# RG-LRU gates: square roots by GpSimd's power, block by block, instead of one ScalarE pass for each scan

## What is computed

```
r, i  = sigmoid(gates of xr)                       # per direction
log_a = -RG_C * r * softplus(-rg_lambda)
a     = exp(log_a)
b     = sqrt(-expm1(2 * log_a)) * (i * xr)
h[t]  = a[t] * h[t-1] + b[t]                       # forwards and backwards
```

## Time and profile before

| | before |
|---|---|
| median of 3 runs | 2858.34 us (2851.83 to 2863.38) |
| the profiled execution | 2857.44 us, span 2855.7 us |
| TensorE busy | 2570.2 us, 90% of the span |
| VectorE busy | 1701.7 us, 60% |
| ScalarE busy | 1007.8 us, 35% |
| GpSimd busy | 445.5 us, 16% |
| mean granted TensorE clock | 0.951 of full speed |

### The profile page before, as it was taken

One profiled execution on the slowest core, in us unless ns is written; L12 is line 12 of the kernel. 1 busy time (PEld: TensorE's weight loads), 2 busy tenths in 40 slices (PEclk: granted clock), 3 DMA queues, 4 the chain that ended last, 5 costly groups with the idle time before them and its releaser, 6 DMA issues.

```text
span 2855.7 us, 37592 instructions
## 1 busy us (share of the span) xinstructions
PE 2570.2 (90%) x14948; PEld 1407.6 (49%) x14948; DVE 1701.7 (60%) x2866; ACT 1007.8 (35%) x1951; POOL 445.5 (16%) x342
## 2 busy tenths in 40 slices
PE   7789999675679898997799799999999999999998
PEld 2344655232376776866445344444444444444443
DVE  5752543767756566745555787787876544444445
ACT  2744443555132232323355533333332222221122
POOL 0400000000653617102233211011110000000000
PEclk8999999887789899998899899999999999999999
DMA  7311111000021222001503434434436412222212
GB/s 209 100 41 41 41 48 27 1 15 22 28 72 46 75 24 69 10 9 60 126 1 126 141 132 140 136 116 140 132 109 239 132 50 81 81 82 81 78 47 72
DMA packets 121625, 227.02 MB, mean 79 GB/s; under 512 B 14281, under 2 KB 59849, under 8 KB 116969
## 3 DMA queue, kind: packets, MB, share of 16 engines
q1 hardware_dynamic: 121448, 224.60, 24.7%
HBM read 162.55 MB, written 61.87 MB: 79 GB/s over the span
## 4 chain that ended last, share of the span: by engine, by line
PE 69%; issue 10%; DVE 8%; POOL 6%; ACT 4%; DMA 1%; SPq 0%; DVEq 0%; POOLq 0%; ACTq 0%
PE pb L2175 23%; PE pb L2117 20%; PE pb L286 8%; PE pb L2097 5%; PE pb L295 2%; POOL arena L1183 2%; POOL arena L1186 1%; DVE arena L1341 1%; POOL arena L1189 1%; PE pb L1776 1%; PE pb L2006 1%; PE pb L525 1%; POOL arena L1207 1%; DVE arena L1443 1%; POOL MS L1200 1%
## 5 line engine op out<-in xcount | busy, mean ns | idle before, releaser
L2175 PE MATMUL pb<-arena 128*128 128x512 f16 x3072 | 667.9, 379 | 0.0
L2117 PE MATMUL pb<-arena 128*128 128x512 f16 (+2 forms) x2736 | 590.6, 378 | 15.2 <-DVE arena L1650 6.6
L2175 PEld LDWEIGHTS pb<-arena 128*128 128x128 f16 x3072 | 300.6, 98 | 362.4
L1740 DVE SCALAR_TENSOR_TENSOR arena<-pb,arena 128x512 f32<-128x512 f32 x512 | 352.2, 690 | 184.6 <-PE pb L2175 183.2
L286 PE MATMUL pb<-arena 128*128 128x512 f16 (+1 forms) x1992 | 423.7, 374 | 21.2 <-ACT arena L970 9.6
L2117 PEld LDWEIGHTS pb<-arena 128*128 128x128 f16 x2736 | 267.9, 99 | 332.9 <-DVE arena L1650 7.1
L286 PEld LDWEIGHTS pb<-arena 128*128 128x128 f16 x1992 | 195.1, 99 | 247.2 <-issue 18.4
L1715 DVE TENSOR_TENSOR arena<-arena,pb 128x512 f32<-128x512 f32 x224 | 149.2, 683 | 251.1 <-PE pb L2117 251.1
L1116 ACT ACTIVATE arena<-arena 128x512 f32<-128x512 f32 x256 | 160.3, 626 | 172.0 <-DVE arena L1715 168.0
L295 PE MATMUL pb<-arena 128*128 128x128 f16 x3264 | 199.7, 222 | 17.3 <-ACT arena L980 11.1
L295 PEld LDWEIGHTS pb<-arena 128*128 128x128 f16 x3264 | 191.9, 99 | 22.4 <-ACT arena L980 11.0
(11 more groups left out here) (292 smaller groups left out, 3192.4 us busy)
## 6 DMA issues: line engine op xcount, KB each, us to landing
arena<-in_mlp_w SPq DMA_DIRECT2D x31, 1024.0 KB, 6.3
w1x<-arena SPq DMA_DIRECT2D x16, 1792.0 KB, 10.6
arena<-w1x SPq DMA_DIRECT2D x16, 1792.0 KB, 9.2
arena<-in_x SPq DMA_DIRECT2D x128, 128.0 KB, 3.8
arena<-in_ada_rest SPq DMA_DIRECT2D x32, 512.0 KB, 3.6
w2x<-arena SPq DMA_DIRECT2D x16, 1024.0 KB, 8.4
arena<-w2x SPq DMA_DIRECT2D x16, 1024.0 KB, 4.9
arena<-in_w_in SPq DMA_DIRECT2D x26, 512.0 KB, 3.9
```

What stands on the lines that cost most here:

```text
L1740: dve.scalar_tensor_tensor(xs, pb[:, 4 + n % 4, :], 1.0 / (WS * AS), xs, ALU.mult, ALU.add).then_inc(S("acc"), 1)
L2117: mm = pe.matmul(pb[:, (7 * g + j) % 4, c], W1P[g % 2][WDEST[a]][0][:, ws, P * k:P * k + P], token_op(b, L // 2, c)[:, k, hs, :], start=(k ...
L2175: mm = pe.matmul(pb[:, 4 + n % 4, :], ACTP[sl][:, 2 * f + th, hs, P * tt:P * tt + P], W2P[sl][:, f, ws, BLK * dh:BLK * dh + BLK], start=(f ...
```

## The change

OM's square root is no longer taken by ScalarE in one pass. GpSimd raises each block of OM to the power 0.5 in place as soon as `rg_om` says that the block is there, and signals `rg_sq` per block (20 times in place of 4). The exponent is a new column `phalf` of 0.5, spread over the block's columns. VectorE multiplies OM by 0.5 * TI block by block too, one block behind: the product of block x - 1 stands behind TI of block x, and the last block's product ahead of the scans. ScalarE's wait for the fifth `rg_om` and its square root are gone.

```diff
@@ kernel scope
+        phalf = sb("phalf", [P, 1])
@@ ScalarE, end of each scan's blocks
-                    act.wait_ge(S("rg_om"), 10 * j + 5 * d + 5)
-                    act.activation(OM, OM, ACT.Sqrt).then_inc(S("rg_sq"), 1)
@@ GpSimd
-            pool.wait_ge(S("pool_init"), 3)
+            pool.memset(phalf[:], 0.5).then_inc(S("pool_init"), 1)
+            pool.wait_ge(S("pool_init"), 4)
...
             pool.memset(view(115, [4 * KB]), 0.0).then_inc(S("rgw_clear"), 1)
+            for v in range(20):
+                b = RORD[v // 5 % 2][v % 5]
+                n, c = (BLK if b < NB else TC), rcols(b)
+                pool.wait_ge(S("rg_om"), v + 1)
+                pool.tensor_tensor(OM[:, c], OM[:, c], phalf[:].broadcast_to([P, n]), ALU.pow).then_inc(S("rg_sq"), 1)
             pool.wait_ge(S("r_rows"), 1)
@@ VectorE
+            def times_root(v, d, x):
+                c = rcols(RORD[d][x])
+                dve.wait_ge(S("rg_sq"), v + 1)
+                ch(dve.scalar_tensor_tensor(OM[:, c], OM[:, c], 0.5, TI[:, c], ALU.mult, ALU.mult))
...
                         ch(dve.scalar_tensor_tensor(TI[:, c], TI[:, c], 1.0, XR[:, c], ALU.add, ALU.mult))
-                    dve.wait_ge(S("rg_sq"), 2 * j + d + 1)
-                    ch(dve.scalar_tensor_tensor(OM, OM, 0.5, TI, ALU.mult, ALU.mult))
+                        if x:
+                            times_root(v - 1, d, x - 1)
+                    times_root(10 * j + 5 * d + 4, d, 4)
```

## The result

The changed kernel takes 4269.8 us (median of 4 runs, 4268.84 to 4273.15) against 2857.7 us before: ratio 1.4952, 95% interval 1.4929 to 1.4975. The direction was as forecast, and its order of size, but the time lies 20 us above the range (3850 to 4250) and 130 us above the forecast of 4140.

What follows compares the result with a forecast made beforehand. The RG-LRU's chain from first OM to scan was taken as the bound, with GpSimd's powers filling it: 2857.4 us plus 1236 for the powers and 46 for VectorE's blocking gave 4139, taken as 4140; range 3850 to 4250 us.

Steps and rivals of the forecast that it cites:

- What bounds the kernel: RG-LRU, last gate block to scan: anything added there moves the kernel's end; 16.4 us from first OM to scan.
- The pace of the power: GpSimd's powers: straight line through one and two columns, 140 ns a column, 72.1 us for 512; 0.80 with or without blocking.
- the 1298 us of the forecast: GpSimd's powers in four scans: 4 x 72.1 + 36.3 = 324.6 us per scan.
- a pace above 150 ns: GpSimd's powers: each column costs over 150 ns; chance 0.04.
- without the blocking: Rival 4: VectorE works freely beside GpSimd's powers, 4093 us; shares the 0.80 of the line with or without blocking.
- Blocking for the whole power: VectorE's two-SBUF-operand operations between powers wait for a whole GpSimd power: 11.7 us a scan, 46 us in all.
- Rival 1: GpSimd's five powers per scan run at a sum's pace, 1.6 us for 512 columns; 2848 us; chance 0.03.
- Rival 2 and 3: GpSimd's powers: several columns together, 35 ns a column, 3174 us, chance 0.13; or 360 ns a column, 6.1 ms.
- The signs that I set: GpSimd trace: 512-column powers about 72 us, wrong under 58 or over 77; GpSimd on chain; about six table loads fewer.

Runs made afterwards that it cites:

- the price list: The kernel before, with useless powers of 1 to 512 columns and varied data, exponents and partitions put into GpSimd's idle time; 2859.9 us.
- the run at a sum's pace: The changed kernel with GpSimd multiplying each block by 0.5 instead of raising it to the power 0.5; 2857.4 us, ratio 0.9995 to before.

## Why the prediction was wrong

- **What bounds the kernel: right.** The stretch from the first OM to the scan is on the chain; the 1412 us all lie there.
- **The pace of the power: the term that was mis-sized.** I took the step from one column to two, 140 ns, for the slope of a straight line through 512. The line holds, and its fixed part of 0.41 us too, but from one column to 512 the price list gives (81.92 - 0.55) / 511 = 159.2 ns a column. That makes 4 x 2304 x 0.0192 = 177 us more than the 1298 us of the forecast: 1475, and GpSimd's busy time shows 1476. The step was the difference of two rows from different lines of the kernel (690 and 550 ns), carried over a factor of 511; the error of 19 ns in it, an eighth, is worth 177 us. Measured side by side, one column and two differ by 154 ns. I noted that part of the 140 ns might not be the loop's and widened the range downwards for that; the other sign had a chance of 0.04 (a pace above 150 ns) and little room: without the blocking the range's upper end of 4250 is 157 ns a column.
- **Blocking for the whole power: wrong here.** It had 46 us in the sum and costs none. The rows that it came from show a product of 1024 columns and a sum of 512; even there VectorE was let go 0.2 us ahead of GpSimd's end (held for 1.52 us of 1.72). A power of 512 columns takes 82 us and lets VectorE go after 0.8. Without the blocking the forecast had been 4093, further off; the two errors had opposite signs, so that 4140 is as near as it is by luck. 4093 + 177 = 4270, and 4269.8 is measured. The page SBUF — State Buffer of the Trainium skill, section "Who interferes with whom", has the shared ports locked for the whole instruction. These runs nearly agree for multiplications (in the run at a sum's pace the product is let go at 527.89, and GpSimd's step ends at 528.03), but not for powers of up to 512 columns nor for two-operand operations beside one of 1024, and the measurement decides.
- **Rival 1, the power at a sum's pace:** the run with multiplications shows it 9 us too cheap, 2857.4 in place of 2848. I had left out that a product beside GpSimd takes 0.72 us more, four times a scan.
- **Rival 2 and 3:** no sign of several columns together up to 2304, nor of 360 ns.
- **The signs that I set:** a power of 512 columns over 77 us was to show the prediction wrong, and it takes 81.9. The sixteen and four powers, the chain on GpSimd, the powers that touch (the sign of no blocking) and six table loads fewer (13 in place of 19) came as written.

## What to carry to other kernels

Before an operation goes to GpSimd, get its price by the column from two lengths that are far apart and near the length wanted; a slope from one column and two, read off different lines, was 12% off, which is nothing at two columns and 177 us here. Where the range hangs on one slope it should leave room on both sides. A cheap-looking function on a few columns (0.55 us for one) says nothing on a tile: 512 columns of power cost 82 us where ScalarE's root took 2.1 us for 2304. Work on GpSimd can also hold VectorE: with multiplications in place of the powers these holds (2.9 us a scan) took all of the gain.

## What the runs showed of the hardware that I hadn't expected

- GpSimd's power takes 0.4 us and 159 ns a column from 1 to 2304 columns, with varied and with constant data (18 columns), with exponents 0.5, -0.5, 1 and 2 (64 columns) and on 16 or 128 partitions (64 columns). 1024 columns are 163 us.
- A GpSimd power holds a VectorE operation that starts with it for 1.6 ns a column up to 512 columns, and none that starts later. Above that (640, 768, 1024) a tensor-scalar is held until the power's end, and so is a cast that starts 147 us into one of 1024 columns (18.17 us in place of 1.92); a two-operand operation is held until about 510 columns before the end (82.2 of 163.2 us) and not after. The long powers were run once each.
- A small power beside a VectorE operation with two operands that started first waits for it: 2.8 us for one that takes 0.69.
